# A seven-product scheme for 54 of 88 up-projection panels, with the modulation tiles moved

## The reference

```python
def swiglu(x, w_up, w_down):
    g, u = jnp.split(x @ w_up, 2, axis=-1)
    return (jax.nn.silu(g) * u) @ w_down
...
    ada = silu_c @ w_ada[l] + b_ada[l]          # 9 x 1024 values per layer, for c and for c_ctx
    n = rmsnorm(h, P['norm_g'][l, 0]) * (1 + sc0) + s0
    h = h + 0.5 * g0 * swiglu(n, P['w_ffn_up'][l, 0], P['w_ffn_down'][l, 0])
    ...                                          # token mixer
    n = rmsnorm(h, P['norm_g'][l, 2]) * (1 + sc2) + s2
    h = h + 0.5 * g2 * swiglu(n, P['w_ffn_up'][l, 1], P['w_ffn_down'][l, 1])
```

## Time and profile before

| | us |
|---|---|
| median of 3 runs | 3210.53 (3208.75 to 3211.26) |
| span of the profiled execution | 3212.5 |
| PE busy | 3108.0 (97%), 20540 matmuls |
| PEld busy | 3031.3 |
| DVE busy | 1745.9 (54%) |
| ACT busy | 970.0 (30%) |
| POOL busy | 47.8 |

### The profile page before, as it was taken

How to read it: one execution, slowest core, us unless ns; L and a number is a source line. 1 busy time by engine, 2 the same in 40 slices (tenths; PEclk the granted TensorE clock), 3 DMA queues, 4 the chain that set the end, 5 groups by cost and what they waited for, 6 DMA issues and landing times.

```text
span 3212.5 us, 47873 instructions
## 1 busy us (share of the span) xinstructions
PE 3108.0 (97%) x20540; PEld 3031.3 (94%) x20540; DVE 1745.9 (54%) x2903; ACT 970.0 (30%) x1475; POOL 47.8 (1%) x92
## 2 busy tenths in 40 slices
PE   7999999998999999999999999999899999999998
PEld 4999999988999899999999999999789989999998
DVE  7656666646555655343465565664665555643334
ACT  3422312313444332121232121232244443322222
POOL 0000000000000000000000000000000000000000
PEclk9999999999999999999999999999999999999999
DMA  8255542354222523232223333334512252321221
GB/s 306 85 196 195 233 158 105 138 203 152 72 77 90 196 88 131 86 118 87 98 76 141 132 143 133 141 128 161 217 65 74 94 192 92 118 88 71 79 76 63
DMA packets 77493, 409.63 MB, mean 128 GB/s; under 512 B 8689, under 2 KB 12209, under 8 KB 46562
## 3 DMA queue, kind: packets, MB, share of 16 engines
q1 hardware_dynamic: 58656, 324.56, 27.3%
q0 software_dynamic: 9504, 56.78, 4.6%
q10 hardware_dynamic: 9122, 25.24, 2.1%
HBM read 360.24 MB, written 46.30 MB: 127 GB/s over the span
## 4 chain that ended last, share of the span: by engine, by line
PE 81%; DVE 11%; ACT 4%; issue 3%; DMA 1%; ACTq 0%; DVEq 0%
PE tile_psum L572 38%; PE tile_psum L579 20%; PE tile_psum L926 5%; PE tile_psum L533 3%; PE tile_psum L930 3%; PE misc_psum L498 3%; PE tile_psum L498 2%; PE tile_psum L538 1%; PE tile_psum L791 1%; PE tile_psum L991 1%; DVE h L1813 1%; DVE n_lo L1735 1%; DVE scaled L1718 1%; ACT squares L1250 1%; DMA raw<-in_w_proj 1%
## 5 line engine op out<-in xcount | busy, mean ns | idle before, releaser
L572 PE MATMUL tile_psum<-n_hi,whi 128*128 128x320 f32 x3264 | 744.2, 309 | 4.0 <-issue 2.1
L572 PE MATMUL tile_psum<-n_lo,whi 128*128 128x320 f32 x3264 | 741.9, 309 | 0.0
L572 PEld LDWEIGHTS tile_psum<-n_hi,whi 128*128 128x128 f32 x3264 | 546.4, 188 | 6.8 <-DVE n_lo L1735 4.2
L572 PEld LDWEIGHTS tile_psum<-n_lo,whi 128*128 128x128 f32 x3264 | 547.1, 188 | 0.0
L579 PE MATMUL tile_psum<-n_hi,wlo 128*128 128x320 f32 x3264 | 512.1, 308 | 0.0
L579 PEld LDWEIGHTS tile_psum<-n_hi,wlo 128*128 128x128 f32 x3264 | 486.9, 188 | 0.0
L1644 DVE TENSOR_TENSOR wlo<-raw,whi 128x2048 fp32r<-128x2048 f32 (+1 forms) x172 | 383.0, 2227 | 180.3 <-ACT whi L1175 178.0
L1175 ACT ACTIVATE whi<-raw 128x2048 fp32r<-128x2048 f32 (+1 forms) x172 | 319.0, 1854 | 330.1 <-DMA raw<-in_w_up 179.0
L572 PE MATMUL tile_psum<-x_hi,whi 128*128 128x320 f32 x1408 | 320.0, 309 | 0.0
L572 PE MATMUL tile_psum<-x_lo,whi 128*128 128x320 f32 x1408 | 319.6, 308 | 0.0
L1869 DVE TENSOR_TENSOR hidden<-gate_act,tile_psum 128x320 f32<-128x320 f32 x176 | 85.6, 486 | 374.9 <-ACT gate_act L1287 374.6
(11 more groups left out here) (300 smaller groups left out, 3733.9 us busy)
## 6 DMA issues: line engine op xcount, KB each, us to landing
raw<-in_w_up SPq DMA_DIRECT2D x88, 1024.0 KB, 4.8
w_ada<-in_w_ada SPq DMA_DIRECT2D x128, 512.0 KB, 5.7
raw<-in_w_down SPq DMA_DIRECT2D x32, 1024.0 KB, 4.8
raw<-in_w_gate SPq DMA_DIRECT2D x24, 1024.0 KB, 4.8
whi<-table_keep SPq DMA_DIRECT2D x20, 1024.0 KB, 4.7
wlo<-table_keep SPq DMA_DIRECT2D x20, 1024.0 KB, 7.1
g_keep<-gate_out POOLq DMA_DIRECT2D x48, 320.0 KB, 2.4
gates<-g_keep POOLq DMA_DIRECT2D x16, 960.0 KB, 5.6
```

The lines of the kernel that those rows point to most:

```text
L572: pe.matmul(tps[:, t.s, m, 0:TH], blk(p, m * n + k)[0], (hi, lo)[b][:, k, tok], start=k == 0 and b == 0, stop=False)
```

## The change

Three of the four feed-forwards, (0,1), (1,0) and (1,1), get a new form, `fast_ffn`, with chunks of 4, 6, 6 and 6 up panels (`FAST_CHUNKS`). The first chunk's panels are computed as before; the other 18 by seven products in place of eight (Strassen's scheme in Winograd's form). An up panel is seen as a 2 x 2 matrix of weight blocks (gate or up, rows 0-511 or 512-1023; b0, b1 gate, b4, b5 up, each 512 columns of the panel), the input as a 2 x 2 matrix (rows by token halves).

- **Weights.** DVE makes four block sums by `weight_sum`: b2 = b4 - b0, b4 = b4 - b5, b3 = b0 - b4, b6 = b1 - b3. A panel then has seven blocks; ACT rounds and DVE splits them in four groups, (0,1), (2), (5,6), (3,4), with `fast_group` and `fast_low`.
- **Tokens.** Once per feed-forward, during the first chunk and its down stage, DVE makes four sums of input blocks (`n_sum`, 512 features x 320 tokens each) with high and low parts.
- **Products.** `fast_product` runs 4 blocks x 3 = 12 matmuls of 320 columns into one bank. P1, P6, P7, P4 add up in one bank of `misc_psum`, P5 and P3 in the other, P2 has a bank of `tile_psum`. ACT copies P1, P5 and the state after P6 to SBUF between them (`keep_p1`, `keep_p5`, `keep_u2`); DVE makes the outputs (`fast_sum11`, `fast_sum22`, `fast_sum12`); ACT's two silus and the multiply and parts of hidden follow. The next product in the same bank waits for the copy. PE's order per panel q: P1(q), P2(q), P3(q-1), P5(q), P6(q), P4(q-1), P7(q); the first down pair of a chunk (`head`, `rest`) is started ahead of P3 and P4 of its last panel.
- **Memory.** Inside these chunks raw blocks go round a ring of 17 blocks of 512 columns and high parts round one of 12, the latter the old three slots; the five more raw blocks lie over acc, sq and tn. Loads come in two halves of 512 KB, and each waits for the products that last read its blocks (`RAW_BEFORE`, `HI_BEFORE`). `junk` moves to a free half of `tile_psum` in fast chunks and to sg in down stages.
- **Modulation tiles.** 58 in (0,0), 35 in each of (0,1) and (1,0), none in (1,1). In the two with 35: 1 per step in the first down stage, 2 in the next two, and 1, 0, 1, 0, 1, 0 / 1, 0, 1, 0, 1, 0 / 2, 1, 1, 1, 1, 1 in the three fast chunks.
- **Loads.** Parameters and the rope constants for the second layer's mixer are reloaded before the last down stage of (1,0), since the token sums lie over them.

```diff
+FAST_CHUNKS = [4, 6, 6, 6]
...
+ADA_PLAN = {(0, 0): [0, 0, 2, 2, 2, 2, 2, 2] + [2] * 4 + [2] * 8 + [2] * 4 + [2] * 6 + [1, 1, 0, 0],
+            (0, 1): [0, 0, 1, 1] + [1] * 4 + [1, 0] * 3 + [2] * 4 + [1, 0] * 3 + [2] * 4 + [2] + [1] * 5 + [0] * 4,
...
+            (1, 1): [0] * len(FAST_KINDS)}
...
+                    if name == "P1" and g >= 2:
+                        pe.wait_ge(act21, g - 1)
+                    elif name == "P2" and g >= 2:
+                        pe.wait_ge(sum11, g - 1)
+                    elif name == "P5" and g >= 2:
+                        pe.wait_ge(sum12, g - 1)
+                    elif name == "P6":
+                        pe.wait_ge(sum11, g + 1)
+                    elif name == "P7":
+                        pe.wait_ge(u2_kept, g + 1)
+                    elif name in ("P3", "P4"):
+                        pe.wait_ge(sum22, g + 1)
...
+                if KINDS[p] == "fast":
+                    g = FAST_OF[p]
+                    for half, bs in enumerate(FAST_HALVES):
+                        for each in releases([RAW_BEFORE[p][b] for b in bs]):
+                            sp.wait_ge(*each)
...
+                for q in range(n):
+                    g = g0 + q
+                    if q + 1 < n:
+                        fast_group(g + 1, 0)
+                        keep_p1(g)
+                        fast_group(g + 1, 1)
+                    else:
+                        round_panel()
+                        keep_p1(g)
+                    silu11(g)
+                    if q + 1 < n:
+                        fast_group(g + 1, 2)
+                    else:
+                        round_panel()
+                    keep_p5(g)
+                    keep_u2(g)
+                    if q:
+                        silu21(g - 1)
+                    if q + 1 < n:
+                        fast_group(g + 1, 3)
+                    if q:
+                        hidden_hi(q - 1)
...
+                for q in range(n):
+                    g = g0 + q
+                    if q:
+                        fast_sum22(g - 1)
+                        fast_low(g, 3)
+                    if q > 1:
+                        hidden_lo(q - 2)
+                    if q + 1 < n:
+                        weight_sum(g + 1, 2, 4, 0)
+                        weight_sum(g + 1, 4, 4, 5)
+                        weight_sum(g + 1, 3, 0, 4)
+                    fast_sum11(g)
+                    if q + 1 < n:
+                        weight_sum(g + 1, 6, 1, 3)
+                        fast_low(g + 1, 0)
+                    else:
+                        split_panel()
+                    if q:
+                        fast_sum12(g - 1)
+                    if q + 1 < n:
+                        fast_low(g + 1, 1)
+                        fast_low(g + 1, 2)
+                    else:
+                        split_panel()
+                    ada_step(plan[q])
+                    if q:
+                        hidden(q - 1)
...
+                        if c == 0 and i == 0:
+                            n_sum(3, [(h12, sub, sum_raw[1]), (add, l12)])
+                            n_sum_low(1)
+                        elif c == 0 and i == 1:
+                            n_sum_low(3)
+                        if i == 2:
+                            at[0] += 6
+                            weight_sum(fast[0], 2, 4, 0)
+                            weight_sum(fast[0], 4, 4, 5)
+                            weight_sum(fast[0], 3, 0, 4)
+                            weight_sum(fast[0], 6, 1, 3)
+                            fast_low(fast[0], 0)
+                        elif i == 3:
+                            for k in range(1, 4):
+                                fast_low(fast[0], k)
+                        ada_step(plan[n + i])
```

More of the change, by code:

```diff
@@ new lines, with before, spans @@
+RAW_AT, HI_AT = placed()
+def before(places):
+    last, out = {}, []
+    for p, at in enumerate(places):
+        out.append([last.get(pos) for pos in at])
+        last.update({pos: (p, b) for b, pos in enumerate(at)})
+    return out
+RAW_BEFORE, HI_BEFORE = before(RAW_AT), before(HI_AT)
+def spans(p, bs):
+    out = []
+    for b in bs:
+        r, h = RAW_AT[p][b], HI_AT[p][b]
+        if out and out[-1][1] + out[-1][3] == r and out[-1][2] + out[-1][3] == h and r != 4 * SLOTS:
+            out[-1][3] += 1
+        else:
+            out.append([b, r, h, 1])
+    return out
@@ L427, in program, with release, releases, own_wait @@
         freed = {}
+        def release(of):
+            p, b = of
+            if KINDS[p] == "prepare":
+                return table_kept[PREPARE_OF[p]], 32
+            return freed[of] if KINDS[p] == "fast" else freed[p]
+        def releases(places, but=()):
+            last = {}
+            for of in places:
+                if of is not None:
+                    s_, n_ = release(of)
+                    last[s_.name] = (s_, max(n_, last[s_.name][1]) if s_.name in last else n_)
+            for of in but:
+                if of is not None:
+                    s_, n_ = release(of)
+                    if s_.name in last and last[s_.name][1] <= n_:
+                        del last[s_.name]
+            return list(last.values())
+        def own_wait(p):
+            return [] if KINDS[p] == "kept" else releases(HI_BEFORE[p], RAW_BEFORE[p])
         class Slot:
@@ new lines, in fast_low, with fast_sum11 @@
+            def fast_low(g, n):
+                p = PANEL_OF[g]
+                if n == 0:
+                    dve.wait_ge(sums_made, 4 * g + 4)
+                dve.wait_ge(fast_hi, 4 * g + n + 1)
+                for _, r, h_, k in spans(p, FAST_GROUPS[n]):
+                    ins = dve.tensor_tensor(lo_at(r, k), raw_at(r, k), hi_at(h_, k).bitcast(F32), ALU.subtract)
+                ins.then_inc(fast_lo, 1)
+            def fast_sum11(g):
+                dve.wait_ge(p1_kept, g + 1)
+                dve.wait_ge(product, product_at(g, "P2"))
+                y = sg[:, g % 2, 0:TH]
+                dve.tensor_tensor(y, y, tps[:, slots.tiles % 2, g % 2, 0:TH], ALU.add).then_inc(sum11, 1)
@@ new lines, in fast_sum22, with fast_sum12 @@
+            def fast_sum22(g):
+                dve.wait_ge(p5_kept, g + 1)
+                dve.wait_ge(product, product_at(g, "P7"))
+                y = hf[:, g % 2, TH:T]
+                dve.tensor_tensor(y, y, mps[:, 0, g % 2, 0:TH], ALU.add).then_inc(sum22, 1)
+            def fast_sum12(g):
+                dve.wait_ge(product, product_at(g, "P3"))
+                dve.wait_ge(u2_kept, g + 1)
+                y = hf[:, g % 2, 0:TH]
+                dve.tensor_tensor(y, y, mps[:, 1, g % 2, 0:TH], ALU.add).then_inc(sum12, 1)
```

477 lines of the change are left out of this document (425 added, 52 removed).

## The result

| | before | after |
|---|---|---|
| median, us | 3210.9 (3208.75 to 3211.34) | 3250.05 (3238.22 to 3255.2) |
| span of the profiled execution | 3212.5 | 3247.5 |
| PE busy | 3108.0 | 3046.4 |
| span less PE busy | 104.5 | 201.1 |
| DVE busy | 1745.9 | 2125.2 |

What follows compares the result with a forecast made beforehand. PE's number of matmuls was taken as the bound: 3212.5 - 95.0 (fewer matmuls) + 56 (stalls) + 12 (clock) = 3185.5 us for the span, median 3184; forecast 3160 to 3198, wider range 3132 to 3222.

Steps and rivals of the forecast that it cites:

- What goes: Fast panels: 84 matmuls instead of 96, 95.0 us off PE; one bank per product costs nothing extra.
- What DVE and ACT get: Per fast panel of 12.32 us: DVE 9.5 us, 11.8 with a tile, ACT 6.8; neither the bound by its total.
- Inside a chunk: Fast panels: no wait without a tile, 0.3 us for each of 12 with one, 3.6 us per feed-forward.
- T + 11.8: Fast panel: its modulation tile lands 11.8 us after T, the start of the panel's product P1.
- (B): Rival: tiles land 1 us later, 24 panels lose 2.7 us each with the clock, 3249 us; chance 0.18.
- D1's rounding: ACT, a chunk's last iteration: rounding down panel D1 waits for P4(4), holds back keep_u2, idles PE 2.6 us before P7.
- Where a chunk ends: Fast chunk ends: ACT's order idles PE 2.6 us twice per feed-forward; 0.8 us in the last chunk.
- The 0.8 of sum11: Last fast chunk's end: D0's rounding, a copy and sum11 make PE wait 0.8 us.
- Where a fast chunk begins: DVE late: first chunk 9 us, two later starts 2.2 each, two-tile panel 1.7; last feed-forward 0.7.
- The stalls' sum: PE stalls in the three changed feed-forwards: 24.7 us twice and 6.7 in the last, 56 us.
- The clock: PE's clock falls after twelve stalls of 1.7 us or longer outside first chunks, 1.0 us each: 12 us.
- (C): Rival: the clock falls at each of sixteen long stalls, 27 us instead of 12, 3199 us; chance 0.12.

Runs made afterwards that it cites:

- e9_all: Changed kernel with POOL issuing the tiles from 74 on, D1 behind hidden in ACT's and DVE's lists, one tile in every fast panel: 3131.59 us.
- e5_fifth: Changed kernel with only the tile of each fast chunk's fifth panel issued by SP ahead of D0's weights: 3212.85 us.
- e1_pool: Changed kernel with tiles from 74 on issued by POOL as soon as their buffer is free, instead of by SP behind weight halves: 3183.53 us.
- e7_order: e1_pool with D1's high part behind the last but one panel's hidden_hi on ACT, its low part behind that panel's hidden_lo on DVE: 3154.08 us.

## Why the prediction was wrong, step by step

**What goes: right.** 19892 matmuls. A product takes 1.76 us at full clock: ACT's copies behind P5, P6 and P4 start 1.76 and 1.75 apart in the changed kernel, so by these rows one bank costs no more than two, as the prediction took it.

```profile
1303.54 0.44 ACT L1644 ACTIVATE hidden<-misc_psum 128x320 f32<-128x320 f32 x1 [0.42 <-PE misc_psum L860]
1305.30 0.44 ACT L1634 ACTIVATE hidden<-misc_psum 128x320 f32<-128x320 f32 x1 [1.32 <-PE misc_psum L860]
1307.05 0.44 ACT L1648 ACTIVATE gate_act<-misc_psum 128x320 f32<-128x320 f32 x1 [1.32 <-PE misc_psum L860]
```

**What DVE and ACT get: right.** Neither was the bound by its total, as e9_all shows with a tile in every fast panel.

**Inside a chunk: the step that failed.** It had a tile landing at T + 11.8, and so gave 0.3 us to each of 12 panels with a tile, 3.6 per feed-forward, 7.2 in both. The tiles landed later, at T + 13.9 in the rows above and at T + 17.2 behind D0. P3's waits are 23.8 and 21.9; less those of the two-tile panels (2.55 and 1.30), which have a term of their own, that is 41.9, and P6's waits for sum11 inside the chunks add 4.8: 46.6 us for 7.2.

The walk took one panel as the pattern of all twelve, and three things were wrong with it. The landing: it is put 3.9 to 4.3 us behind the issue, built on the shortest landing in the earlier trace rows, 3.1, and it was 5.1 to 6.3 in the four that I followed. The earlier trace rows had medians of 5.7 and 5.3 for such tiles, set aside because they stood behind a full 1 MB. With 5.7 the walk's tile lands at T + 13.3, 1.5 us later than it was put, and (B) has the whole gain gone at 1.1 us a panel: the prediction's own rows left its sign open. The chunk's first panel: its P3 comes seven products behind P1, not nine, so at T + 12.3, and the tile that landed at T + 10.7 cost 1.36. The fifth panel: its tile stands behind D0, whose blocks P3(3) and P4(3) give back, and it is issued at T + 11.0 and 11.5. The prediction named D1's rounding as late for that same reason, on ACT, and didn't follow the same panels through SP's list. These six cost 27.4 us of stalls and, by e5_fifth, 37 in all.

**Where a chunk ends: the stalls right, the forecast of their cause half.** keep_u2 came 2.38 or 2.47 us late in the second and third chunks of all three, against 2.6 forecast. The 0.8 of sum11 in the last chunk shows in (1,1) alone, 0.82. In the last chunk of (1,0) and (1,1) there was a third stall, 2.76 and 2.09, which I had not: ACT stood at D1's transfer, 3.87 and 3.19 us. In (1,1):

```profile
3183.05 1.48 ACT L1482 ACTIVATE whi<-raw 128x1536 fp32r<-128x1536 f32 x1 [3.19 <-DMA raw<-in_w_down]
```

So ACT does take its list strictly in order, as the step had assumed, and the Trainium skill ("Perfetto Trace Analysis", section "Tensor Engine Instruction") says of its queue; an ACT that passes a waiting instruction would have shown none of this. What the step left out is that DVE's list has the same panel ahead of hidden: with ACT's cured, x_lo came 2.0 to 3.3 us late in (1,1), and nothing was gained.

**Where a fast chunk begins: right.** 1.17 + 1.58 and 0.55 + 1.66 for the forecast 2.2 each; the two-tile panel 2.55 and 1.30 for 1.7; the first chunk 2.85 + 3.88 + 1.98 = 8.7 for 9; (1,1) 1.0 for 0.7. The ten more tiles of (0,0) cost nothing, as forecast.

**The stalls' sum.** 96.6 more idle time for 56. PE's waits of the three feed-forwards add up to 101, 45 more than forecast, and the rest of the kernel idles some 4 us less than before. Of the 45 the panels with a tile bear 39, the third ACT stalls 5 and x_lo 2; the other terms are within 2 us of their forecast.

**The clock: 33.4 for 12.** It was priced with the stalls I had, twelve at 1.0; with 27.4 us more in six long ones there were more falls: in stretches of 2 us the clock goes low sixteen times in (0,1) and (1,0) and once in (1,1), so a fall costs 33.4/17 = 2.0 us, where I had 1.7. By the stretches most falls cost 1.7 and four of the six behind the long waits 3.4. Rival (C), a fall at each long stall, is not what happened: of 25 waits of 1.7 us or more 16 brought the clock down, among them all seven of 3.9 and more. The Trainium skill ("TensorE: Matmul & The Clock Gate", section "HAM oscillation") has PE throttled again at each wait of a series, with waits of about 3 to 5 us; this trace agrees for the seven waits of 3.9 us and more, and the shorter ones, which (C) counted on, lie outside that example.

**The rivals.** (B), late tiles, was the mechanism, given 0.18. That its number fits, 2.7 us for each of 24 panels, 3249 against 3250, is luck: it has 24 us of stalls and 41 of clock, where the trace has 39 and 21 over the forecast, and its even spread was wrong, since a quarter of the panels bore 27.4 of the 45.7 us of stalls. With the tiles in time e1_pool measured 3184, the forecast's number; here too two errors meet, 47 us more idle time for 56 and 22 of the clock for 12. The rest of the sum stood to within some 10 us a term, and one term carried the sign.

## What to carry to other kernels

When work is added that brings its own transfers, follow every one of them through the issuing queue, and name what the transfer ahead of it waits for; do it for the first and the last iteration of a loop too, not for the middle one alone. Before reordering one engine's list to remove a stall, look whether a second engine has the same piece ahead of the same product: here the two gates stood in a row, and only removing both paid. Where an engine in order waits for a transfer, issuing that transfer one place earlier is a cheap experiment; here it was worth 2%.

## What the runs showed of the hardware that I had not expected

A short idle time of PE doesn't always bring the clock down, and its length alone doesn't decide. Of the changed kernel's eight waits for keep_u2 three brought it down (2.47, 2.38 and 2.38 us) and five did not (2.38, 2.47, 2.76, 2.47 and 2.09). Behind 2.38 us in one chunk of (0,1), and behind 2.47 us in the same place of the next (us, PE busy, granted clock, DMA share, GB/s):

```profile
1355.00:1357.00 2.00, 1.65 (x11) 1.00 0.77 292
...
1487.00:1489.00 2.00, 1.78 (x7) 0.58 0.65 258
1489.00:1491.00 2.00, 2.00 (x10) 0.57 0.04 15
```

In e7_order waits of 1.98, 1.57, 1.66 and 1.64 us in (0,1) all passed at full clock. The earlier trace rows has a fall behind 1.16 us, but there six matmuls of 2 columns follow the wait, so PE did next to nothing for longer than the 1.16 us that the prediction reads. What decides it for a wait of 1 to 3 us these runs don't settle. A 512 KB transfer behind other halves took 6.3 us to land in a feed-forward whose DMA engines were 0.31 busy on average; in e1_pool, at 0.33, the same transfers had a median of 4.3. The mean share says little of how long one transfer takes.
